# Gates folded into the experts' results, and the two rows of a token added by the second gather

## The chip, the core and the metric

The kernel runs on one core of a Trainium2 chip. The time is the device time of one execution in microseconds; the median of three executions of the kernel before is 1756.83 us (1756.41 to 1758.56). The engines are TensorE (PE in the profile; PEld is its loading of weights), VectorE (DVE), ScalarE (ACT), GpSimd (POOL) and SyncE (SP). POOL issues the indirect DMAs (gathers), SP and ACT issue the others.

## The reference

One layer of a model with 1024 tokens of width 1024: four attention-like branches, and then a mixture of 32 experts. The change concerns the mixture and the norm behind it:

```
h2 = rmsnorm(x2);  each token: a group by argmax, its two best experts e0, e1
gates g0, g1 = softmax(top 2) * softmax(group)          # per token
ys[e, slot] = (silu(h2 @ w1[e]) * (h2 @ w3[e])) @ w2[e]    # for the tokens of e
x2 = x2 + g0 * ys[row of (token, e0)] + g1 * ys[row of (token, e1)]
out = rmsnorm(x2) * final_norm_g
```

## The kernel before

All is float32; a matmul of the expert phase is made of three passes on values split in a high part (fp32r) and the remainder. `CAP` = 96 tokens of an expert form its block; tokens beyond 96 go to overflow blocks, whose code stands in a branch that is not taken with these inputs (`overflow`, L2461 on). The 32 experts are passed two at a time: experts 0 and 1 and experts 30 and 31 in code of their own, the others in a loop (`loop`, L2455). For an expert `e` = 2i + j:

- POOL copies the expert's token numbers and gathers 96 rows of `h2_rows` (`xg`); TensorE transposes them; ScalarE and VectorE make `xT_hi`, `xT_lo`.
- SP loads the weights; ScalarE makes the high part of each quarter, VectorE the remainder (`wa_lo` L2768, `wb_lo` L2776).
- TensorE runs the up projection in four quarters (`up`, 12 matmuls each), later the down projection (`down`, 24 matmuls). In between are ScalarE's sigmoid, VectorE's two products (`gl`, `hid`, L2762, L2764), TensorE's transposes of `hid` (L2410), and the split `hT_hi`, `hT_lo`.
- ScalarE copies the 96x1024 result from PSUM to `yo` (`y_out`, L2687) and stores it in `ys`, a DRAM tensor with 96 rows for each expert. For the last expert, 31, the down projection is done in two halves of 512 columns (L2564), each copied and stored at once (`y_end`).

VectorE works out where each token's two results lie (`blocks_of_experts` and what follows it); these row numbers are in `row_of`, and they hold overflow blocks too. The order on each engine is that of the code; there is no scheduler. Engines wait for one another by semaphores (`wait_ge`, `then_inc`), and `link` makes VectorE wait for its own last instruction.

`combine` is the end. POOL waits until every block is stored and then issues 16 gathers of 128 rows of 1024: for each tile `t` of 128 tokens one for the first expert (`ya`) and one for the second (`yb`). VectorE adds each to `x2[t]` multiplied by its gate (L2945, L2947). ScalarE squares and sums the tile (L2926) and takes the root (L2929); VectorE, after it has added the next tile, takes the reciprocal and multiplies by it and by the gain `fg` (L2938, L2939); SP stores the tile (L2906).

Of the kernel before, what the change touches and what calls it, by code (L numbers as in the profile page):

```python
# [49 lines left out]
SLOTS = (NE + N_OV) * CAP  # L50
# [42 lines left out]
def build(nc, a):  # L93

    ctx = ExitStack()
    with ctx:
# [89 lines left out]
        s.ys = dram("ys", [SLOTS, DM])  # L186
# [23 lines left out]
        s.row_of = sb("row_of", [P, 2 * NT], 202.125, I32)  # L210
        s.tok_of = sb("tok_of", [CAP, NE + N_OV], 202.25, I32)
        s.totals = sb("totals", [P, NE], 203)
        s.asg = sb("asg", [P, 8, 2, NT], 203.125)
        s.late_ready, s.routed = sem("late_ready"), sem("routed")
        s.late = {n: sb("late_" + n, shape, at) for n, shape, at in (
# [814 lines left out]
def attend(nc, a, s):  # L1030
# [136 lines left out]
    with nc.Block() as block:  # L1167
        @block.sync
        def _(sp):
# [16 lines left out]
            for k in range(2 * NGT):  # L1186
# [6 lines left out]
                if k in range(16, 30, 2):  # L1193
                    at = NE + (k - 16) // 2 * N_OV // 7
                    sp.wait_ge(zeros_ready, 1)
                    sp.dma_start(s.ys[at * CAP:(at + N_OV // 7) * CAP, :].rearrange("(b p) n -> p b n", p=CAP),
                                 zeros[:, :].unsqueeze(1).to_broadcast([CAP, N_OV // 7, DM])).then_inc(zeros_stored, 16)
                if k == 9:
                    sp.dma_start(bias[:, :, :], bass.AP(s.shifted.tensor, P - 1,
                                                        [[NH * 768 - 1, P], [768, NH], [1, BAND]])).then_inc(bias_in, 16)  # L1200
# [11 lines left out]
                if k == 56:  # L1212
                    sp.wait_ge(zeros_stored, 16 * 7)
# [656 lines left out]
def route(nc, a, s):  # L1870
# [24 lines left out]
    hot = sb("r_hot", [P, 2, NT, NE], 178)  # L1895
    both, cum = sb("r_both", [P, NT, NE], 180), sb("r_cum", [P, NT, NE], 181)
# [135 lines left out]
    def vector(dve):  # L2032
# [178 lines left out]
        nc.vector.tensor_copy(s.totals[:, :], psum[:, 4, 0:NE]).then_inc(s.routed, 1)  # L2211

# [122 lines left out]


# [3 lines left out]
def experts(nc, a, s):  # L2340
# [22 lines left out]
    OVER = 3  # L2363
    ov_set, over_ready, over_used, over_tok = sem("ov_set"), sem("over_ready"), sem("over_used"), sem("over_tok")
# [13 lines left out]
                                      "hid", "hT", "hT_taken", "y", "y_taken", "stored")}  # L2378
# [82 lines left out]
    def overflow(eng, body, before=None):  # L2461
# [3 lines left out]
        with eng.If(blocks > 0):  # L2465
            if before is not None:
                before()
            with eng.Fori(0, N_OV) as b:
                body(b)

    def expert_of(eng, b):
        return eng.value_load(s.ov_i[0:1, 0, bass.ds(b, 1)], min_val=0, max_val=NE - 1)

    def sync(sp):
# [15 lines left out]
        refill(NE // 2, 0, False, True)  # L2490

        def before():
            sp.wait_ge(ov_table, 1)
            sp.wait_ge(b_used, 2 * NE)

# [9 lines left out]
    def gpsimd(pool):  # L2505
# [16 lines left out]

        def before():
            pool.wait_ge(over_tok, 1)
            pool.wait_ge(b_used, 2 * NE)
            pool.sem_inc(ov["go"], 1)

# [7 lines left out]
        overflow(pool, body, before)  # L2535
        for j in range(2):
            pool.wait_ge(y_stored[j], 16 * (NE // 2 + j))

    def tensor(pe):
# [45 lines left out]
        def body(i, j, start, last):  # L2585
# [10 lines left out]
            if start:  # L2596
                pe.wait_ge(xT_low, 1)
                up(i, j, 2)
            if not last:
# [13 lines left out]
        down(NE // 2 - 1, 1, False, end=True)  # L2613

# [30 lines left out]
    def scalar(act):  # L2645
# [26 lines left out]
        def y_end(i):  # L2672

            act.wait_ge(y_stored[1], i * 16)
            for h in range(2):
                act.wait_ge(b_used, i * 4 + 3 + h)
                half = slice(h * 512, (h + 1) * 512)
                nc.scalar.activation(yo[1][:, half], y_banks(True)[:, h, :], ACT.Copy).then_inc(y_half, 1)
                act.wait_ge(y_half, h + 1)
                act.dma_start(s.ys[(i * 2 + 1) * CAP:(i * 2 + 2) * CAP, half], yo[1][:, half]).then_inc(y_stored[1], 16)  # L2680
# [11 lines left out]
        def body(i, j, start, last):  # L2692
# [32 lines left out]
            if last:  # L2725
                y_out(i, 0, False)
# [10 lines left out]
        y_end(NE // 2 - 1)  # L2737

        def before():
            for j in range(2):  # L2740
                act.wait_ge(y_stored[j], 16 * (NE // 2 + j))

        def body(b):
# [10 lines left out]
            act.dma_start(s.ys[bass.ds((b + NE) * CAP, CAP), :], yo[0][:, :]).then_inc(ov["stored"], 16)  # L2754
        overflow(act, body, before)

    def vector(dve):
# [28 lines left out]
        def blocks_of_experts():  # L2786
# [8 lines left out]
            link(nc.vector.tensor_tensor(cnt[:, 0, :], cnt[:, 2, :], cnt[:, 0, :], ALU.subtract))  # L2795
            some = many[:, 0:2 * NT, :]
            link(nc.vector.tensor_tensor(some, line(0).unsqueeze(2).to_broadcast([P, 2 * NT, MORE]),
                                         late["steps"][:, :].unsqueeze(1).to_broadcast([P, 2 * NT, MORE]),
                                         ALU.is_ge))
            link(nc.vector.tensor_reduce(out=line(3), in_=some, axis=AX.X, op=ALU.add))  # L2800
            link(nc.vector.scalar_tensor_tensor(out=line(4), in0=line(3), scalar=-float(CAP), in1=line(0),
                                                op0=ALU.mult, op1=ALU.add))
            link(nc.vector.tensor_scalar(line(6), line(3), 1.0, None, ALU.min))
            every = [P, 2 * NT, NE]
            link(nc.vector.tensor_tensor(hot2[:, :, :], late["e"][:, :].unsqueeze(1).to_broadcast(every),
                                         line(1).unsqueeze(2).to_broadcast(every), ALU.is_equal))
# [206 lines left out]
```

## Time and profile before

| | |
|---|---|
| median of three runs | 1756.83 us |
| the profiled execution | 1755.01 us |
| its span (first to last instruction of the profile) | 1753.2 us |
| TensorE busy | 1682.4 us, 96% |
| VectorE busy | 1440.0 us, 82% |
| ScalarE busy | 938.5 us, 54% |
| POOL busy | 137.5 us, 8% |
| chain of waits: TensorE's L2548 and L2580, the expert projections | 20% and 10% of the span |
| the expert phase, by the first matmul of expert 0 | from about 1140 us |

A profile is one execution recorded by the hardware. A busy share is an average over phases with different limits. The chain of waits goes back from the last instruction to whatever released it; it tells which engine set the end. A timeline row gives start, length, engine, line, operation, and the tiles written and read; in square brackets stands how long the engine had been idle and what released it. Ends of matmuls are modelled: a record of 0.39 us belongs to matmuls that start 0.23 us apart.

### The profile page before, as it was taken

To read this page: it belongs to the slowest core of one execution; us is meant where nothing else is said; L and a number is where in the kernel's file an instruction comes from. 1 tells how busy PE (TensorE), PEld (TensorE's weight loads), DVE (VectorE), ACT (ScalarE), POOL (GpSimd) and SP (SyncE) were. 2 spreads that over 40 slices of the span, in tenths; PEclk is the share of its full clock that TensorE was granted. 3 is DMA by queue.
4 is the path that set the end of the run, shared out by engine and by line. 5 is a ranking of instruction groups with operands and counts; after the bars stand their busy time and mean duration, and the time that the engine had idled before them with its cause. 6 is when DMAs were issued, how large, how long until landed. Compare 5 with 4: busy or idle time off the path is not lost. (4 is left out here: it accounts for less than half of the span.)

```text
span 1753.2 us, 24115 instructions
## 1 busy us (share of the span) xinstructions
PE 1682.4 (96%) x8776; PEld 1271.4 (73%) x8776; DVE 1440.0 (82%) x2045; ACT 938.5 (54%) x1218; POOL 137.5 (8%) x137
## 2 busy tenths in 40 slices
PE   7999999999999999999999999999999999999990
PEld 7768888877777777777777778867777777777760
DVE  6587958989789988678737986789998989898997
ACT  6533122133444555545566542177778787777762
POOL 1100000000000000000000000032212111100003
PEclk9999999999999999999999999999999999999995
DMA  5202122122354412412315942399999999999977
GB/s 210 72 1 85 54 103 97 61 79 79 111 193 124 147 61 67 144 55 69 124 37 199 329 167 83 121 381 392 402 395 405 393 404 394 403 395 403 402 281 287
DMA packets 77040, 359.82 MB, mean 205 GB/s; under 512 B 9020, under 2 KB 11612, under 8 KB 50588
## 3 DMA queue, kind: packets, MB, share of 16 engines
q1 hardware_dynamic: 67372, 325.14, 49.7%
q0 software_dynamic: 5888, 20.97, 3.6%
q10 hardware_dynamic: 3696, 12.59, 1.8%
q8 instruction: 53, 0.87, 0.2%
q14 instruction: 31, 0.25, 0.0%
HBM read 301.63 MB, written 55.99 MB: 204 GB/s over the span
## 5 line engine op out<-in xcount | busy, mean ns | idle before, releaser
L2768 DVE TENSOR_TENSOR wa_lo<-wa,w_hi 128x2048 fp32r<-128x2048 f32 x124 | 280.9, 2283 | 14.8 <-ACT w_hi L2652 14.1
L2652 ACT ACTIVATE w_hi<-wa 128x2048 fp32r<-128x2048 f32 x124 | 237.6, 1917 | 75.8 <-DMA wa<-expert_up 54.5
L1583 PE MATMUL psum<-h_hi,w_hi 128*128 128x512 f32 x512 | 210.4, 411 | 2.1 <-ACT gate_out L1245 1.6
L1583 PE MATMUL psum<-h_hi,w_lo 128*128 128x512 f32 x512 | 204.3, 399 | 0.0
L1583 PE MATMUL psum<-h_lo,w_hi 128*128 128x512 f32 x512 | 202.3, 395 | 0.0
L175 DVE MAX8 top<-sel 128x8 f32<-128x384 f32 (+5 forms) x192 | 171.2, 892 | 4.6
L173 DVE MATCH_REPLACE8 sel<-top,sel 128x384 f32<-128x384 f32 (+5 forms) x192 | 168.1, 875 | 0.0
L2776 DVE TENSOR_TENSOR wb_lo<-wd,w_hi 128x2048 fp32r<-128x2048 f32 x62 | 139.3, 2288 | 30.6 <-ACT w_hi L2662 30.6
L2548 PE MATMUL psum<-w_hi,xT_hi 128*96 128x512 f32 x508 | 162.1, 400 | 0.0
L2548 PE MATMUL psum<-wa_lo,xT_hi 128*96 128x512 f32 x512 | 159.8, 393 | 0.0
L2548 PE MATMUL psum<-w_hi,xT_lo 128*96 128x512 f32 x508 | 158.6, 393 | 0.0
L1583 PEld LDWEIGHTS psum<-h_hi,w_hi 128*128 128x128 f32 x512 | 96.3, 188 | 49.9 <-issue 16.8
L1262 ACT ACTIVATE pt<-psum 128x512 f32<-128x512 f32 (+3 forms) x144 | 61.1, 470 | 116.5 <-PE psum L1603 116.4
L2662 ACT ACTIVATE w_hi<-wd 128x2048 fp32r<-128x2048 f32 x62 | 116.0, 1909 | 0.7 <-PE psum L2548 0.5
L969 PE MATMUL psum<-h_hi,w_hi 128*128 128x512 f32 x288 | 115.0, 399 | 0.0
L1583 PEld LDWEIGHTS psum<-h_hi,w_lo 128*128 128x128 f32 x512 | 96.2, 188 | 24.8 <-issue 5.1
L969 PE MATMUL psum<-h_hi,w_lo 128*128 128x512 f32 x288 | 112.5, 391 | 0.0
L969 PE MATMUL psum<-h_lo,w_hi 128*128 128x512 f32 x288 | 112.2, 390 | 0.0
L1583 PEld LDWEIGHTS psum<-h_lo,w_hi 128*128 128x128 f32 x512 | 96.4, 188 | 19.8 <-issue 2.7
L2548 PEld LDWEIGHTS psum<-wa_lo,xT_hi 128*96 128x96 f32 x512 | 82.6, 161 | 35.5
L2548 PEld LDWEIGHTS psum<-w_hi,xT_lo 128*96 128x96 f32 x508 | 82.1, 162 | 35.2
L2548 PEld LDWEIGHTS psum<-w_hi,xT_hi 128*96 128x96 f32 x508 | 77.4, 162 | 27.0 <-issue 0.2
(398 smaller groups left out, 3296.6 us busy)
## 6 DMA issues: line engine op xcount, KB each, us to landing
wa<-expert_up SPq DMA_DIRECT2D x128, 1024.0 KB, 23.4
wd<-expert_down SPq DMA_DIRECT2D x64, 1024.0 KB, 23.6
w<-w_gate SPq DMA_DIRECT2D x32, 512.0 KB, 4.2
gate_pre<-gate_out SPq DMA_DIRECT2D x64, 256.0 KB, 3.5
gate<-gate_pre SPq DMA_DIRECT2D x32, 512.0 KB, 5.9
ys<-yo ACTq DMA_DIRECT2D x31, 384.0 KB, 7.0
w<-w_T SPq DMA_DIRECT2D x18, 512.0 KB, 3.7
ys<-zeros SPq DMA_DIRECT2D x7, 1152.0 KB, 5.9
```

The costliest lines, as they stand in the source:

```text
L173: link(nc.vector.match_replace(sc, top8[:, :], sc, TAKEN))
L175: link(nc.vector.max(top8[:, :], sc))
L969: ins = nc.tensor.matmul(psum[:, bank + h, :], w[:, k, :], x[:, k, h * 512:(h + 1) * 512], start=(k == 0 and r == 0), stop=(k == KC - 1 an ...
L1262: nc.scalar.activation(dst, src, ACT.Copy).then_inc(pt_copied, 1)
L1583: ins = nc.tensor.matmul(psum[:, 7, :], w[:, k, :], x[:, k, half * 512:(half + 1) * 512], start=(n == 0), stop=(n == BURST - 1))
L2548: ins = nc.tensor.matmul(psum[0:CAP, up_bank(i, j) + m, :], x[:, k, :], w[:, c, m, :], start=(k == 0 and x is xT_hi[j] and w is not wa_lo[ ...
L2652: nc.scalar.activation(hi_a(i, j, q).rearrange("p c m n -> p (c m n)"), wa[j][q][:, :, :, :].rearrange("p c m n -> p (c m n)"), ACT.Copy). ...
L2662: nc.scalar.activation(dst.rearrange("p f n -> p (f n)"), wb[j][q][:, :, :].rearrange("p f n -> p (f n)"), ACT.Copy).then_inc(b_high, 1)
L2768: nc.vector.tensor_tensor(wa_lo[j][q][:, :, :, :].rearrange("p c m n -> p (c m n)"), wa[j][q][:, :, :, :].rearrange("p c m n -> p (c m n)" ...
L2776: nc.vector.tensor_tensor(wb_lo[j][q][:, :, :].rearrange("p f n -> p (f n)"), wb[j][q][:, :, :].rearrange("p f n -> p (f n)"), high.rearra ...
```

## The change

1. *Gates.* At the end of the routing VectorE multiplies the one-hot table of each token's experts by the gates and splits it in two (`hot_g`). TensorE sums it over the tokens with 16 small matmuls (`slot_gates`), and the result, `slot_gate`, holds for each expert and each of its 96 slots the gate of the token there. ScalarE's copies of results out of PSUM now multiply by it.
2. *Row numbers.* They are worked out early, before VectorE's last weight subtractions, and only for the first 96 tokens of experts 0 to 29 (`early_rows`). A token whose expert is 30 or 31, or that has overflowed, gets the number of a row of zeros. Overflow blocks have a tensor of their own, `ys_ov`, gathered and added inside the branch that is not taken.
3. *Gathers.* POOL issues eight gathers for the tokens' first experts into eight buffers `rows_of`, as soon as expert 29 is stored and the buffer is free, then eight for the second experts, which add to the same buffers in memory (`compute_op=ALU.add`).
4. *Experts 30 and 31* (`LATE` = 2) are not stored. ScalarE writes the high part of the gated result (`yl_hi`), VectorE the remainder (`yl_lo`), and TensorE puts them in their tokens' places by one-hot matrices `hotT` that compare a running number with the expert's token numbers: eight matmuls of 512 columns a tile.
5. *Sums.* VectorE adds TensorE's tile from PSUM to `x2[t]`, and then the buffer `rows_of[t]`. For tiles 2 and 3 (`ON_PE`) TensorE adds the buffer instead, by two plain float32 matmuls with the identity, so that VectorE adds once.
6. *The end.* All eight tiles are summed before the first is multiplied. The gain is loaded and the square root's table set earlier; `out` has buffers of its own.

```diff
         def body(i, j, start, last):          # pool: behind the loop
+        pool.wait_ge(a_used, 4 * (NE - 1))
+        pool.iota(tok_iota[:, 0:ZERO_ROW], ...)
+        pool.iota(tok_iota[:, ZERO_ROW:], ...).then_inc(iota_set, 1)
+        s.set_eps(pool)
+        pool.wait_ge(s.rows_set, 1)
+        for j in range(2):
+            pool.wait_ge(y_stored[j], 16 * (NE // 2 - 1))
+        for k in range(2):
+            for t in range(NT):
+                ...
+                if k:
+                    pool.wait_ge(s.rows_in[t], 16)
+                    pool.indirect_dma_start(rows_of[t][:, :], None, s.ys, at, compute_op=ALU.add
+                                            ).then_inc(s.rows_in[t], 16)
+                else:
+                    if t >= 2:
+                        pool.wait_ge(a_used, 4 * (NE - 1) + (2 if t < 6 else 3))
+                    pool.indirect_dma_start(rows_of[t][:, :], None, s.ys, at).then_inc(s.rows_in[t], 16)
...
+        def late(t, k):                        # tensor
+            for h in range(2):
+                if t == 0:
+                    pe.wait_ge(late_low, k + 1 + k * h)
+                for r, y in enumerate((yl_hi[k], yl_lo[k])):
+                    ins = nc.tensor.matmul(psum[:, late_banks(t) + h, :], hotT[k][:, t * P:(t + 1) * P],
+                                           y[:, h * 512:(h + 1) * 512], ...)
+            if k == LATE - 1 and t in ON_PE:
+                pe.wait_ge(s.rows_in[t], 32)
+                for h in range(2):
+                    ins = nc.tensor.matmul(psum[:, late_banks(t) + h, :], s.ident[:, :],
+                                           rows_of[t][:, h * 512:(h + 1) * 512], start=False, stop=True)
+            if k == LATE - 1:
+                ins.then_inc(late_ready, 1)
+        late(0, 0)
+        late(1, 0)
+        late(0, 1)
+        late(1, 1)
+        for t in range(2, NT):
+            if t >= 4:
+                pe.wait_ge(s.summed if t - 4 in ON_PE else late_taken, t - 3)
+            for k in range(LATE):
+                late(t, k)
...
-            nc.scalar.activation(yo[j][:, :], y_banks().rearrange("p a b -> p (a b)"),
-                                 ACT.Copy).then_inc(y_taken, 1)
+            nc.scalar.activation(yo[j][:, :], y_banks().rearrange("p a b -> p (a b)"), ACT.Copy,
+                                 scale=s.slot_gate[:, bass.ds(i * 2 + j, 1)]).then_inc(y_taken, 1)
...
+        def late_adds():                       # vector
+            taken = 0
+            for t in range(NT):
+                dve.wait_ge(late_ready, t + 1)
+                at = late_banks(t)
+                ins = nc.vector.tensor_tensor(s.x2[t][:, :], psum[:, at:at + 2, :].rearrange("p a b -> p (a b)"),
+                                              s.x2[t][:, :], ALU.add)
+                if t in ON_PE:
+                    ins.then_inc(s.summed, 1)
+                    continue
+                taken += 1
+                ins.then_inc(late_taken, 1)
+                dve.wait_ge(late_taken, taken)
+                dve.wait_ge(s.rows_in[t], 32)
+                nc.vector.tensor_tensor(s.x2[t][:, :], rows_of[t][:, :], s.x2[t][:, :], ALU.add
+                                        ).then_inc(s.summed, 1)
...
-        for t in range(NT):                    # combine, vector
-            x2 = s.x2[t][:, :]
-            dve.wait_ge(y_in[t], 32)
-            link(nc.vector.scalar_tensor_tensor(out=x2, in0=ya[t][:, :], scalar=s.gates[:, 0, t:t + 1], in1=x2,
-                                                op0=ALU.mult, op1=ALU.add))
-            link(nc.vector.scalar_tensor_tensor(out=x2, in0=yb[t][:, :], scalar=s.gates[:, 1, t:t + 1], in1=x2,
-                                                op0=ALU.mult, op1=ALU.add))
-            nc.vector.engine_nop().then_inc(summed, 1)
-            if t:
-                finish(t - 1)
-        finish(NT - 1)
+        for t in range(NT):
+            dve.wait_ge(rooted, t + 1)
+            link(nc.vector.reciprocal(rms[:, t:t + 1], rms[:, t:t + 1]))
+            nc.vector.scalar_tensor_tensor(out=out[t][:, :], in0=s.x2[t][:, :], scalar=rms[:, t:t + 1],
+                                           in1=fg[:, :], op0=ALU.mult, op1=ALU.mult).then_inc(final, 1)
```

On VectorE, the end of the program before: `x` is the tile of the running sum, `ya` and `yb` the gathered rows.

```order
L2945 SCALAR_TENSOR_TENSOR x_0_9500<-ya_10668,gates,x_0_9500 128x1024
L2947 SCALAR_TENSOR_TENSOR x_0_9500<-yb_10676,gates,x_0_9500 128x1024
L2949 ISA
L2945 SCALAR_TENSOR_TENSOR x_1_9501<-ya_10669,gates,x_1_9501 128x1024
L2947 SCALAR_TENSOR_TENSOR x_1_9501<-yb_10677,gates,x_1_9501 128x1024
L2949 ISA
L2938 RECIPROCAL rms_10687<-rms_10687 128x1
L2939 SCALAR_TENSOR_TENSOR ya_10668<-x_0_9500,rms_10687,fg 128x1024
```

The same place on VectorE in the changed program, behind the last difference `yl_lo` of expert 31; `rows_of` are the gathered buffers.

```order
L2951 SCALAR_TENSOR_TENSOR yl_lo_10686<-psum,slot_gate,yl_hi_10676 96x512
L2960 TENSOR_TENSOR x_0_9502<-psum,x_0_9502 128x1024
L2969 TENSOR_TENSOR x_0_9502<-rows_of_10677,x_0_9502 128x1024
L2960 TENSOR_TENSOR x_1_9503<-psum,x_1_9503 128x1024
L2969 TENSOR_TENSOR x_1_9503<-rows_of_10678,x_1_9503 128x1024
L2960 TENSOR_TENSOR x_2_9504<-psum,x_2_9504 128x1024
L2960 TENSOR_TENSOR x_3_9505<-psum,x_3_9505 128x1024
L2960 TENSOR_TENSOR x_4_9506<-psum,x_4_9506 128x1024
L2969 TENSOR_TENSOR x_4_9506<-rows_of_10681,x_4_9506 128x1024
```

Two gated additions and a product per tile have become two plain additions (one for tiles 2 and 3), and the products stand behind all of them.

On POOL, the end of the program before, from the last gather for the loop to the first four of the end.

```order
L2508 DMA xg_9545<-h_rows,idx_10658 96x1024
L2464 TENSOR_LOAD ov_i
L2464 ISA x2
L2465 COMPARE_AND_BRANCH
...
L2911 MEMSET eps_10688 128x1
L2916 DMA ya_10668<-ys,row_of 128x1024
L2916 DMA yb_10676<-ys,row_of 128x1024
L2916 DMA ya_10669<-ys,row_of 128x1024
L2916 DMA yb_10677<-ys,row_of 128x1024
```

And in the changed program; L2605 are the plain gathers, L2600 those that add.

```order
L2570 DMA xg_9549<-h_rows,idx_10663 96x1024
L2587 IOTA tok_iota 96x768
L2588 IOTA tok_iota 96x256
L2525 MEMSET eps_10692 128x1
L2605 DMA rows_of_10677<-ys,row_of 128x1024
L2605 DMA rows_of_10678<-ys,row_of 128x1024
L2605 DMA rows_of_10679<-ys,row_of 128x1024
...
L2600 DMA rows_of_10677<-ys,row_of 128x1024
L2600 DMA rows_of_10678<-ys,row_of 128x1024
...
L2508 TENSOR_LOAD ov_i
L2508 ISA x2
L2509 COMPARE_AND_BRANCH
```

The 16 gathers have moved ahead of the overflow branch and of the stores of experts 30 and 31, and the two of a tile no longer stand side by side: all plain ones come first.

## Rows read from the trace of the kernel before

**Rows 1.** Chain that ended last, from 1690: start us, us, what

```profile
1701.01 5.58 PE psum L2564 x24
...
1711.53 5.36 DMA yb<-ys,row_of
...
1716.99 1.29 DVE x L2945
```

**Rows 2.** Timeline, one tile near the end: start us, us, engine, line, operation, tiles

```profile
1738.69 0.16 DVE L2938 RECIPROCAL rms<-rms 128x1 f32<-128x1 f32 x1
...
1738.89 1.28 DVE L2939 SCALAR_TENSOR_TENSOR ya<-x,rms,fg 128x1024 f32<-128x1024 f32 x1
...
1748.52 1.28 DVE L2939 SCALAR_TENSOR_TENSOR ya<-x,rms,fg 128x1024 f32<-128x1024 f32 x1
```

**Rows 3.** The tile out, its last two stores

```profile
DMA to landing us min/median/max: 2.9/3.1/3.3
```

**Rows 4.** Windows: from:to, length, busy us by engine, granted clock, DMA share, GB/s

```profile
1710.00:1710.50 0.50, 0.00 (x0) 0.00 (x0) 0.00 (x0) 0.00 (x0) 0.24 (x1) 0.89 0.00 0
...
1720.00:1724.00 4.00, 0.00 (x0) 0.00 (x0) 3.77 (x5) 3.85 (x7) 3.09 (x4) 0.50 1.01 407
```

**Rows 5.** Timeline, VectorE, TensorE at expert 31's down projection

```profile
1696.94 0.69 DVE L2764 TENSOR_TENSOR hid<-psum,gl 96x512 f32<-96x512 f32 x1
1697.55 2.28 DVE L2776 TENSOR_TENSOR wb_lo<-wd,wa_lo 128x2048 fp32r<-128x2048 f32 x1
1697.69 0.55 PE L2410 MATMUL psum<-ident,hid 96*128 96x96 f32 x4
```

**Rows 6.** Timeline of VectorE before and after it

```profile
1689.36 4.50 DVE L2776 TENSOR_TENSOR wb_lo<-wd,w_hi 128x2048 fp32r<-128x2048 f32 x2 [0.62 <-ACT w_hi L2662]
1693.78 2.28 DVE L2776 TENSOR_TENSOR wb_lo<-wd,wa_lo 128x2048 fp32r<-128x2048 f32 x1
...
1700.22 0.48 DVE L2788 TENSOR_TENSOR l_many<-totals,late_steps 128x320 f32<-128x320 f32 x1
```

**Rows 7.** Groups by form, VectorE and TensorE: count, busy us, mean ns

```profile
L2039 DVE TENSOR_TENSOR x<-psum,x 128x512 f32<-128x512 f32 x16 | 11.0, 691 | 17.3 <-PE psum L1701 17.3
L2768 DVE TENSOR_TENSOR wa_lo<-wa,w_hi 128x2048 fp32r<-128x2048 f32 x124 | 280.9, 2283 | 14.8 <-ACT w_hi L2652 14.1
L177 DVE TENSOR_SCALAR sel<-sel 128x1024 f32<-128x1024 f32 x1 | 0.7, 694 | 0.0
L1524 PE MATMUL psum<-k,q 64*128 64x512 f32 x88 | 24.3, 637 | 0.0
```

**Rows 8.** The tile ys, the store of expert 29 at 1686.6

```profile
DMA to landing us min/median/max: 7.0/7.0/7.0
```

**Rows 9.** Timeline, VectorE and POOL at two places

```profile
1162.92 4.48 DVE L2776 TENSOR_TENSOR wb_lo<-wd,w_hi 128x2048 fp32r<-128x2048 f32 x2
1163.39 4.83 POOL L2508 DMA_INDIRECT xg<-h_rows,idx  x1 [0.80 <-POOL idx L2517]
...
1717.74 1.35 POOL L2916 DMA_INDIRECT ya<-ys,row_of  x1 [0.31 <-issue]
1718.31 1.28 DVE L2947 SCALAR_TENSOR_TENSOR x<-yb,gates,x 128x1024 f32<-128x1024 f32 x1
...
L2916 POOL DMA_INDIRECT yb<-ys,row_of x8 | 8.0, 997 | 2.4 <-issue 2.4
```

**Rows 10.** Timeline of ScalarE, last half of expert 31

```profile
1706.61 0.59 ACT L2678 ACTIVATE yo<-psum 96x512 f32<-96x512 f32 x1 [2.13 <-PE psum L2564]
```

**Rows 11.** Timeline of TensorE near the program's start

```profile
13.59 0.43 PE L839 MATMUL psum<-w_lo,h_hi 128*128 128x268 f32 x1
...
17.39 0.29 PE L839 MATMUL psum<-w_hi,h_hi 128*128 128x268 f32 x1
```

**Rows 12.** Timeline of TensorE, first two experts

```profile
1148.48 0.63 PE L2548 MATMUL psum<-w_hi,xT_lo 128*96 128x512 f32 x2
1150.96 0.88 PE L2404 MATMUL psum<-ident,xg 96*128 96x96 f32 x8 [1.85 <-DMA xg<-h_rows,tok_of]
```

More of the change, by code:

```diff
@@ L2334, in tensor, with slot_gates @@
         s.late_tokens = late_tokens
+        def slot_gates():
+            pe.wait_ge(s.gates_set, 1)
+            for k in range(2):
+                for t in range(NT):
+                    ins = nc.tensor.matmul(psum[0:CAP, 3, 0:2 * NE], hot_c[:, k, t, :],
+                                           hot_g[:, k * NT + t, :, :].rearrange("p r e -> p (r e)"),
+                                           start=(k == 0 and t == 0), stop=(k == 1 and t == NT - 1))
+            ins.then_inc(s.gates_summed, 1)
+        s.slot_gates = slot_gates
     return Engines(sync=sync, gpsimd=gpsimd, scalar=scalar, vector=vector, tensor=tensor)
@@ L2534, in body @@
             pool.sem_inc(ov["go"], 1)
-        overflow(pool, body, before)
-        for j in range(2):
-            pool.wait_ge(y_stored[j], 16 * (NE // 2 + j))
+        overflow(pool, body, before, then)
     def tensor(pe):
@@ L2736, in scalar @@
         loop(act, body)
[L2737 to L2741, printed above, removed]
+        y_late(1)
+        nc.scalar.activation(table[:, :], s.totals[:, 0:1], ACT.Sqrt)
         def body(b):
@@ L2801, in blocks_of_experts, with late_rows @@
-            link(nc.vector.scalar_tensor_tensor(out=line(4), in0=line(3), scalar=-float(CAP), in1=line(0),
-                                                op0=ALU.mult, op1=ALU.add))
[L2803 to L2806, printed above, removed]
+        def late_rows():
+            link(nc.vector.tensor_copy(tok_f[:, :], s.tok_of[:, NE - LATE:NE]))
+            dve.wait_ge(iota_set, 1)
+            for k in range(LATE):
+                nc.vector.tensor_scalar(hotT[k][:, :], tok_iota[:, :], tok_f[:, k:k + 1], None, ALU.is_equal
+                                        ).then_inc(late_hot, 1)
@@ L2881, in body, with then @@
             glu(ov["half"], b + 1).then_inc(ov["hid"], 1)
-        overflow(dve, body, before)
+        def then():
+            for n in range(2 * NT):
+                t, k = n // 2, n % 2
+                dve.wait_ge(ov_in[k], 16 * (t + 1))
+                if k:
+                    dve.wait_ge(ov_added, n)
+                nc.vector.scalar_tensor_tensor(out=s.x2[t][:, :], in0=ov_rows[k][:, :],
+                                               scalar=s.gates[:, k, t:t + 1], in1=s.x2[t][:, :], op0=ALU.mult,
+                                               op1=ALU.add).then_inc(ov_added, 1)
+            dve.wait_ge(ov_added, 2 * NT)
+        overflow(dve, body, before, then)
     return Engines(sync=sync, gpsimd=gpsimd, tensor=tensor, scalar=scalar, vector=vector)
```

231 lines of the change are left out of this document (164 added, 67 removed).

## The prediction, made before the result was known

> **What bounds the kernel now.** I read the page's busy shares first, then the chain of waits, and last the timeline of the final 60 us. TensorE is 96% busy, and inside the expert loop the chain never leaves it: up to the last matmul of expert 31 the time is TensorE's. That ends when 24 matmuls of the last down projection, 0.2325 us apart, have run (1701.01 + 5.58 = 1706.6) [rows 1]. Then come two things that are not TensorE's. First a gap of 10.4 us: the result is copied and stored, POOL starts its 16 gathers only after that store, and the first pair is there when the chain leaves the second gather, begun at 1711.53 and 5.36 us long, so VectorE starts at 1716.99 [rows 1]. Then VectorE alone: 8 tiles in 1749.80 - 1716.99 = 32.8 us, of which the reciprocal and the last product are 1740.17 - 1738.69 = 1.48 us a tile, and the two gated additions are the rest, 2.6 us a tile [rows 2]. After 1748.52 + 1.28 = 1749.80 the last store takes 3.3 us [rows 3]; the span ends 3.4 us after VectorE. So 46.6 us of the 1753.2 lie behind TensorE's last matmul, and all that the change can win is there.
>
> **The change, part by part.**
>
> *Start of the experts.* VectorE gets four instructions behind the totals (two of 256, two of 512 elements, at most 0.69 us each by the 512-element addition [rows 7], so under 2.5 us), and TensorE 16 small matmuls behind expert 0's third quarter. TensorE stands there anyway: it is through with the quarter at about 1149.1, and the next instruction begins at 1150.96, 1.85 us later, waiting for rows of expert 1 [rows 12]. At the price of the eight transposes behind that wait (8 in 0.88 [rows 12]) 16 take 1.8 us. Cost 0; bounds 0 and 0.9 us, half of them uncovered. VectorE's two quarters move from 1143.7 to 1146 and are needed at 1151.6 and later: nothing. ScalarE's copies only gain a scale operand: nothing, it waits elsewhere.
>
> *Row numbers for experts 0 to 29.* Five dependent instructions of 16 elements before VectorE's last subtractions; at a reciprocal's 0.16 us plus a gap of 0.04 [rows 2] they take 1.0. The subtraction behind them waited 0.62 us for ScalarE [rows 6], so VectorE is 0.4 late; the subtraction of 1693.78 ended at 1696.06, and the two products that end in the gated rows began about 1696.2, so 0.15 of that is absorbed [rows 5, 6]. TensorE's transposes begin at 1697.69, right behind that product's end at 1697.63 [rows 5], and nothing else is in its queue ahead: TensorE's end moves by 0.3, to 1706.9. Bounds 0 and 0.4.
>
> *Experts 30 and 31 no longer go through memory.* Behind TensorE's end come ScalarE's half copy, 0.59 [rows 10], and VectorE's difference, 0.7, but TensorE fills that time: it owes tiles 0 and 1 their expert 30 part first. 8 matmuls of 0.2325 bring it to 1708.8, four more finish tile 0 at 1709.7 plus a tail of 0.16, and VectorE can begin at 1709.9 instead of 1716.99. TensorE has tiles 1 and 2 (without its rows) done at 1712.5. The block count (first instruction 0.48 [rows 6]) stands between VectorE's two half differences, under a half projection of 12 x 0.2325 = 2.8 us: free.
>
> *VectorE's own work.* An addition of 1024 elements: between 691 ns at 512 and 2283 ns at 2048 [rows 7], that is 1.22, with its gap 1.25. There are 14 (two a tile, one for tiles 2 and 3): 17.5 us. Products with reciprocal: 8 x 1.48 = 11.8. Together 29.3 against 32.8. All sums now come before the first product, so the root of a tile is long there; the stores then come every 1.48 us, and the last two stores of before, that close together, landed after 2.9 to 3.3 us [rows 3]. I keep 3.4.
>
> *The gathers.* Here lies the price that decides. All 16 are issued by POOL as before; eight plain, then eight that add. The first waits for expert 29's store, issued at 1686.6 and landed 7.0 us later, at 1693.6 [rows 8]. Unhindered, a gather is 1.0 us with 0.3 between two [rows 9]. But in the loop POOL's gather begun at 1163.39 lasts 4.83 us: it ends at 1168.2, one gather's length after VectorE's pair of subtractions ends at 1167.40. In the tail the gather begun at 1717.74 is only 1.35 long, though a 1.28 us product starts at 1718.31 and isn't stretched [rows 9]. I read: a gather that begins inside a VectorE instruction with two operands in SBUF waits for a gap between two such, and once begun holds nobody up. By that reading the first gather waits for the subtraction of 1693.8, now 0.4 later, until 1696.5 and ends at 1697.4; the second ends at 1698.7; the third waits for the last weight subtraction until 1700.1 and ends at 1701.0; the fourth for the two one-hot comparisons (0.69 each [rows 7]) until 1702.4; the next four follow at 1.3. The first adding gather is issued at 1708.8 and, at 5.4 to landing [rows 1], is there at 1714.2; those of tiles 1, 2, 3 at 1715.5, 1716.8, 1718.1.
> A rule of the Trainium skill stands beside this reading (SBUF — State Buffer, section "SBUF: two separate sides"): VectorE with two SBUF inputs and a GpSimd instruction that reads SBUF take a shared port pair exclusively, for the whole instruction, whoever is first. The wait for VectorE agrees with 4.83 us; the other half, VectorE held for a whole gather, does not, since its products stay at 1.28 us in the midst of the gathers, and by it the end would come up to 8 us later than below, if each of the eight late gathers held VectorE for 1.0.
>
> *The sum.* VectorE adds tile 0's sum from 1709.9 to 1711.2 and waits for rows until 1714.2. Then tile 0 to 1715.5, tile 1 to 1718.0. Tile 2's rows come through TensorE by an identity: a plain float32 matmul of 512 columns is 637 ns long in the record [rows 7], so 0.47 apart if its tail is the usual 0.16; two end at 1717.8, and VectorE is done at 1719.2. TensorE has tile 3 at 1717.8 + 1.9 + 0.94 = 1720.6, VectorE takes it to 1722.0; tile 4 is ready at 1722.6, and four tiles at 2.5 end at 1732.6. With 11.8 and 3.4 the span ends at 1747.8, against 1753.2. In one line: VectorE starts 7.1 us earlier, has 3.5 less work, and loses 5.1 in waits (3.0 for tile 0's rows, 1.5 and 0.6 for tiles 3 and 4), so about 5.4 are gained. The profiled execution is 1755.01, 1.8 above its span and 1.8 below the median of 1756.83; the difference carries over: 1756.83 - 5.4 = 1751.4.
> Bounds. Below: no gather is held up and rows are never late; tile 3 is then ready at 1712.5 + 0.94 + 1.9 + 0.94 + 0.16 = 1716.4, tile 4 at 1718.2, VectorE's last addition ends at 1728.2 and the span at 1743.4. Above: TensorE idles from 1712.5 to 1716.8. In the profile its clock fell about 3.8 us after the last matmul (1706.6 to the half-lowered stretch 1710.0 to 1710.5 [rows 4]). At 1.2 GHz its prices double; at the start of the program matmuls that began at 13.2 without a pause were long, 0.43, until 17.2 and 0.29 from then [rows 11], so I take 4 us of the low level: tile 3 is 1.9 later, the end 1749.7.
>
> **Rivals.**
> *Gathers in time.* If POOL's waits are rarer than I think, the lower bound holds: 1756.83 - 9.8 = 1747.0. For it: in the tail only a few tenths were lost per gather. Against: 4.83 us in the loop, and three subtractions of that kind in POOL's way.
> *TensorE stays at the low level.* Tile 2's two take 1.9 then, to 1718.7; tile 3's eight 3.7 and its two 1.9, to 1724.3; after it a tile comes every 3.7 us, tile 7 at 1739.1; end 1739.1 + 2.5 + 11.8 + 3.4 = 1756.8, time 1760.4. For it: the gap in which it falls. Against: from there on TensorE works without a pause.
> *The other side: a gather that adds is much dearer than a plain one.* No row shows one. At 407 GB/s and full DMA share [rows 4] half a megabyte is 1.3 us; bounds for one that adds are 1.3, the plain price, and 3.9, if reading the rows, reading the buffer and writing it came one after another. The first lands at 1716.5 then, the eighth 7 steps later, and VectorE adds it, 1.25, before the products. From a step of 2.9 us on the kernel is slower than before; at 3.9 the end is 1743.8 + 1.25 + 11.8 + 3.4 = 1760.3, the time 1763.9. At 2.6 (1758.3) it is still no change. I take 1.3, since the eight can overlap and at that price they keep ahead of VectorE's 2.5 us a tile.
>
> **How the numbers follow.** My forecast 0.45 (its own range 1749 to 1755), gathers in time 0.30, low clock throughout 0.08, dear adding gathers 0.17, a third of it at 2.6 or less. A measurement tells 0.2%, 3.5 us, from no change: faster means under 1753.3. Nine tenths of the forecast and all of the second: 0.69. Slower, over 1760.3: most of the dear gathers and half of the low clock, 0.15; the rest 0.16. Range 1745 to 1760.
>
> **What would show it.** Right: TensorE's last projection ends near 1706.9; VectorE's first addition from PSUM near 1710 and a wait of 2 to 4 us for an adding gather behind it; eight plain gathers on POOL, two or three of 2 to 3 us; the product phase 11.8 us long and all in one piece. Wrong: VectorE waits for adding gathers at tiles 4 to 7 too (they are dear), or for TensorE at each tile (clock), or additions stretched above 1.3 us, or the expert loop longer than before.

## The result, and the profile after

The changed kernel takes 1760.56 us (median of 20 runs), the kernel before 1757.75 (20 runs): ratio 1.0014, 95% interval 1.0008 to 1.0020. It is a little slower, inside the 0.2% that I had called no change, and above my range of 1745 to 1760. The profiled execution has a span of 1761.0 us. One of the changed kernel's 20 executions took 5956 us, which nothing here explains; it is left out of the ratio and doesn't move the median.

The 7.8 us between the two spans lie in two places. Take the end of TensorE's last projection product, by its record, as the mark: in the kernel before it was at 1706.6 (1701.01 + 5.58 [rows 1]), 46.6 us ahead of the end of the span. After:

```profile
1712.96 0.39 PE L2656 MATMUL psum<-wa_lo,xT_lo 128*96 128x512 f32 x1
1713.19 0.40 PE L2714 MATMUL psum<-yl_hi,hotT 96*128 96x512 f32 x1
```

These are rows of the timeline (start, duration, engine, line, operation). The last projection product ends at 1713.35, 6.8 us later than before; the first product of the late experts follows it without a gap. From the mark to the end it is 47.7 us, where I had forecast 40.9 and the kernel before has 46.6.

**Ahead of the experts.** This is the granted clock in the routing stage (windows: TensorE busy, instructions, clock, DMA share, GB/s):

```profile
1126.00:1130.00 4.00, 4.00 (x22) 1.00 0.33 98
1134.00:1138.00 4.00, 4.00 (x22) 0.50 0.87 367
1142.00:1146.00 4.00, 4.00 (x24) 0.50 1.00 414
1146.00:1150.00 4.00, 4.00 (x13) 0.50 0.76 280
1150.00:1154.00 4.00, 4.00 (x17) 0.90 0.68 198
```

From about 1134 to 1151 TensorE ran at its lower level, 1.2 GHz (0.50). In the profiled execution of the kernel before it stayed at 2.4 GHz:

```profile
1140.00:1144.00 4.00, 4.00 (x23) 1.00 1.02 408
1144.00:1148.00 4.00, 4.00 (x19) 1.00 1.02 368
```

There [rows 12] show TensorE waiting 1.85 us for the rows of expert 1. In the chain of waits after, there is no such wait:

```profile
1146.76 10.33 PE psum L2640 x36
1157.09 1.31 PE psum L2359 x16
1158.40 0.72 PE psum L2448 x8
```

The 36 products of the up projection run into the 16 gate products (L2359), and those into the transposes: the gate products are 1.31 us of the path.

**Behind the experts.** The waits between 1705 and 1750 (engine, tile and line, released by, total, times, longest):

```profile
PE psum L2720 <- DMA rows_of<-ys,row_of: 8.5, 1, 8.5
DVE x L2960 <- PE psum L2720: 7.5, 2, 5.1
DVE x L2969 <- DMA rows_of<-ys,row_of: 4.9, 1, 4.9
```

VectorE waits 4.9 us for tile 0's rows and 7.5 us for TensorE, which itself stood 8.5 us for tile 2's rows. The chain of waits through it:

```profile
1718.01 9.23 DMA rows_of<-ys,row_of
1727.25 0.04 issue
1727.29 3.78 PE psum L2720 x4
1731.07 1.92 PE psum L2714 x8
1732.99 1.72 PE psum L2720 x4
1734.71 1.85 PE psum L2714 x8
1736.58 1.24 DVE x L2960
...
1746.67 0.17 DVE rms L3124
```

Tile 2's adding gather starts at 1718.01, its rows are there 9.2 us later. The identity products (L2720, four records a tile) then take 3.78 us for tile 2 and 1.72 for tile 3. The gathers on POOL:

```profile
1699.28 2.37 POOL L2605 DMA_INDIRECT rows_of<-ys,row_of  x1 [13.13 <-DMA ys<-yo]
1701.95 1.87 POOL L2605 DMA_INDIRECT rows_of<-ys,row_of  x1 [0.30 <-issue]
1704.13 3.21 POOL L2605 DMA_INDIRECT rows_of<-ys,row_of  x1 [0.30 <-issue]
...
1713.00 0.94 POOL L2605 DMA_INDIRECT rows_of<-ys,row_of  x1 [0.30 <-issue]
1714.25 1.59 POOL L2600 DMA_INDIRECT rows_of<-ys,row_of  x1 [0.30 <-issue]
1716.14 1.56 POOL L2600 DMA_INDIRECT rows_of<-ys,row_of  x1 [0.30 <-issue]
```

On POOL a plain one is 0.94 long when nothing holds it up, one that adds 1.55. What follows lies in the DMA engines, by the windows while nothing but adding gathers runs:

```profile
1722.00:1724.00 2.00, 0.00 (x0) 0.50 1.04 207
1724.00:1726.00 2.00, 0.00 (x0) 0.50 1.08 215
```

At full DMA share the adding gathers deliver 207 to 215 GB/s, half of what the plain gathers of [rows 4] do at 407.

### The profile page after: what moved, and what is told of

It is laid out like the page before. It is cut to its first block and busy times, and to the rows that moved or that the text cites. A ratio compares the mean times of both kernels' runs of the same rounds, so it can differ in the third digit from the quotient of the medians.

```text
span 1761.0 us, 24321 instructions
## 1 busy us (share of the span) xinstructions
PE 1711.3 (97%) x8864; PEld 1293.3 (73%) x8864; DVE 1438.1 (82%) x2042; ACT 947.3 (54%) x1221; POOL 170.1 (10%) x139
```

## The experiments

Theory: the tail is long because adding gathers take the DMA engines twice as long and land late, and because tiles 2 and 3 go through TensorE. The rival was that the time was lost upstream by the clock. Each median is of 5 to 12 runs, and each ratio is to runs of the kernel before taken beside them: 35 (medians 1757.72, 1757.94) or 17 (1757.37). "Tail" is from the mark to the end of the span, in the one profiled execution of each; the changed kernel's first profile had 47.7. A and B below are the theory and the rival of each experiment's own expectation.

| kernel | median us | ratio to before | tail us |
|---|---|---|---|
| before, again | 1757.08 | 0.9994 (0.9985 to 1.0003) | 46.6 |
| changed, again | 1759.52 | 1.0009 (1.0000 to 1.0017) | 47.0 |
| vector_adds_all | 1754.82 | 0.9985 (0.9976 to 0.9994) | 44.1 |
| plain_second_gather | 1757.12 | 0.9997 (0.9988 to 1.0006) | 45.1 |
| gathers_interleaved | 1757.43 | 0.9991 (0.9982 to 1.0000) | 44.5 |
| interleaved_vector_adds | 1756.38 | 0.9984 (0.9975 to 0.9992) | 43.2 |
| one_gate_product | 1758.99 | 1.0006 (0.9997 to 1.0015) | 48.0 |
| tensor_kept_busy | 1758.29 | 1.0003 (0.9994 to 1.0012) | 45.5 |
| standstills_filled | 1758.69 | 1.0010 (1.0001 to 1.0019) | 50.1 |
| half_the_adding | 1752.48 | 0.9965 (0.9953 to 0.9977) | 41.0 |
| half_the_adding_odd | 1752.16 | 0.9965 (0.9952 to 0.9979) | 40.2 |

**The kernel before, again** (no edit).

> The kernel before, once more, for its granted clock. Theory A (the fall of TensorE's clock to 0.50 between 1134 and 1150 us, which cost the profiled execution of the changed kernel 6.9 us, comes now and then in either kernel): this look may show it or not; the mean granted clock of its executions scatters from 0.983 to 0.988, and the slowest are those with the lowest clock. Rival B (only the changed kernel has it): the clock is 1.00 from 1120 to 1160 us again, and all executions have 0.988.

Its windows:

```profile
1134.00:1138.00 4.00, 3.06 (x28) 1.00 0.81 340
1138.00:1142.00 4.00, 4.00 (x23) 0.52 0.94 307
1142.00:1146.00 4.00, 4.00 (x18) 0.50 1.01 422
1146.00:1150.00 4.00, 4.00 (x14) 0.70 0.88 297
```

The low level is here too, from 1138 to about 1148, and TensorE's last projection ends at 1709.4, 2.8 us later than in the first profile, with the same tail. So B is out: the kernel before has the fall as well. Of the 35 executions of the kernel before that ran beside it, two have a mean granted clock of 0.988, the value of the execution that I had studied, with spans of 1752.4 and 1752.9; the other 33 have 0.981 to 0.987 and 1754.1 to 1760.2. That the profile I predicted from was a rare one fits this, and the 1.8 us by which it lay under the median; how rare isn't shown, for a mean counts falls anywhere, and this execution has another one (granted clock 0.86 from 456 to 460 us and 0.71 from 460 to 464). Of the 13 profiled executions here, nine have the fall in the routing stage.

**VectorE adds all rows.**

```
-    ON_PE = (2, 3)
+    ON_PE = ()
```

> The changed kernel, but VectorE also adds the gathered rows of tiles 2 and 3 (two additions of 1.23 us more), and TensorE has no identity product. Theory A (the tail is long because tile 2's rows come late and their price on TensorE is 3.8 us at the low clock, and tiles 3 and 4 queue behind that): VectorE waits for rows at tile 0 only, then runs 16 additions in one piece, last addition 4 to 5 us earlier against TensorE's last projection, time 0.2 to 0.3% under the changed kernel. Rival B (the adding gathers' own pace is the bound, about 2.5 us from landing to landing): VectorE waits again at tiles 2 and 3 for rows, and no more than 1 us is won. Rival C (the time is set upstream, by TensorE's low clock in the routing stage, and the tail hardly counts): the time stays within 1 us of the changed kernel's unless the granted clock from 1132 to 1150 us stays at 1.00.

The time is 5.7 and 4.7 us under the changed kernel's two medians, at A's upper end or above it, and the tail 2.9 to 3.6 shorter. VectorE waited four times for rows:

```profile
DVE x L2969 <- DMA rows_of<-ys,row_of: 7.2, 4, 6.3
```

Tile 0 is 6.3 of it, the other three 0.9 in all. From then on the rows come just as fast as VectorE adds, and the DMA engines are full all the while, at half the rate of a plain gather:

```profile
1725.00:1727.00 2.00, 2.00 (x10) 1.00 1.06 211
1727.00:1729.00 2.00, 1.12 (x5) 1.00 1.06 211
1729.00:1731.00 2.00, 0.00 (x0) 1.00 1.06 211
```

512 KB at 211 GB/s are 2.48 us a gather. So A is right on TensorE's detour and on what is won, and B on the gathers' pace alone. The profiled execution had no clock fall in the routing stage; the 16 gate products then lie in a wait for expert 1's rows, of which 1.5 us are left, and TensorE's last projection ended at 1708.0, 1.4 later than in the first profile of before, since those rows came 1.5 later.

**The second gather plain.**

```
-                    pool.indirect_dma_start(rows_of[t][:, :], None, s.ys, at, compute_op=ALU.add
+                    pool.indirect_dma_start(rows_of[t][:, :], None, s.ys, at
```

> The changed kernel, but the second gather of each tile overwrites the buffer instead of adding to it, so the first expert's row of each token is left out of the sum. Theory A (a gather that adds is the dear thing: 1.55 us on POOL against 0.94, and some 8 us from issue to landing against 5.4): POOL's second eight are 0.94 long with 0.3 between, tile 0's rows are there 5.4 us after the issue, so VectorE's wait at tile 0 falls from 4.9 to about 2.5 us and TensorE's for tile 2's rows from 8.5 to about 4; the end comes 3 to 5 us earlier. Rival B (the landing is late because VectorE or the weight loads' traffic hold the gathers, whatever they do with the buffer): the second eight land as late as before, 8 to 9 us after issue, and the time is the same.

```profile
1717.00:1719.00 2.00, 0.00 (x0) 0.56 1.02 418
1719.00:1721.00 2.00, 0.00 (x0) 0.50 1.02 412
```

Double the rate at the same share: 1.25 us a gather. The tail is 45.1 against 47.0 and 47.7: 1.9 to 2.6 us for the adding, less than A's 3 to 5. One part of A fell: the first of these gathers (issued at 1711.43) served VectorE only at 1718.6, 7.1 us later; VectorE's wait at tile 0 was 5.3, not 2.5, and TensorE's for tile 2 was 6.3, not 4. The first adding gather of the changed kernel took 8.1 (1714.25 to 1722.33), so most of what is over 5.4 isn't the adding.

**Another order on POOL.**

```
+        order = ((0, 0), (0, 1), (0, 2), (0, 3), (1, 0), (1, 1), (0, 4), (1, 2), (0, 5), (1, 3), (0, 6), (1, 4),
+                 (0, 7), (1, 5), (1, 6), (1, 7))
+        for k, t in order:
```

> The changed kernel with another order on POOL: plain gathers of tiles 0 to 3, then adding and plain ones in turn (tile 0, 1, then 4, 2, 5, 3, ...), so that tile 0's adding gather is issued about 5 us earlier. Theory A (an adding gather has a latency of 8 us, and the wait for the first is what is lost): VectorE's wait at tile 0 goes from 4.9 to under 1 us, TensorE's wait for tile 2's rows from 8.5 to about 4 us, and the time falls by 3 to 5 us. Rival B (the engines of the DMA rings are the bound, 16 gathers and the last stores sharing them): the last rows land no earlier, and VectorE only waits at a later tile; under 1 us.

VectorE's wait at tile 0 is gone, TensorE's for tile 2 is 5.2 instead of 8.5. The median is 3.1 and 2.1 us under the two of the changed kernel: A, at its lower end or just under it.

**Both edits together.**

> The changed kernel with both edits of the first experiments: POOL issues adding gathers in turn with the later plain ones, and VectorE adds the rows of all eight tiles. Theory A (an adding gather occupies the DMA engines for 2.46 us where a plain one takes 1.25, so the 16 need some 30 us of them; VectorE's 16 additions and 8 products are the other limit): rows of tile 0 are there when TensorE's sum is, VectorE waits 2 to 4 us in all for later rows, from TensorE's last projection to the end of the span 39 to 41 us against 47.7 of the changed kernel, 44.0 and 44.5 of the two single edits; time 6 to 8 us under the changed kernel and 3.5 to 5 under the kernel before. Rival B (latency of each adding gather, not the engines' time): no wait behind the first tile, 38 us. Rival C (both single edits removed the same wait): 43 to 44 us.

Rival C: 43.2, no faster in the median than VectorE's adding alone. VectorE waits for rows at five tiles, and POOL, ahead of four adding gathers, for the plain gather into the same buffer:

```profile
DVE x L2970 <- DMA rows_of<-ys,row_of: 6.3, 5, 2.1
POOL rows_of L2601 <- DMA rows_of<-ys,row_of: 7.3, 4, 2.2
```

VectorE's sum is only 0.9 under the 7.2 above. POOL's waits leave the DMA engines no gap, though; from 1714 to 1734 their share is 1.02 or more in every stretch of 4 us, as in this one (here the busy time is VectorE's):

```profile
1722.00:1726.00 4.00, 2.36 (x2) 1.00 1.05 277
```

So an earlier first gather hardly brings the last rows earlier.

**One gate product instead of 16.**

```
-            for k in range(2):
-                for t in range(NT):
-                    ins = nc.tensor.matmul(psum[0:CAP, 3, 0:2 * NE], hot_c[:, k, t, :],
+            ins = nc.tensor.matmul(psum[0:CAP, 3, 0:2 * NE], hot_c[:, 0, 0, :],
```

> The changed kernel with one product for the slots' gates at the start of the experts instead of 16, so all gates but those of token tile 0's first choice are left out. Theory A (where TensorE's clock falls to 0.50 in the routing stage, its wait for rows of expert 1 is used up, and the 16 products cost their whole 1.31 us): with such a fall, from the start of the products of oh_late to the first transposes of expert 0's hidden rows it takes 1.2 us less than in the changed kernel at the same fall, about 26.0 instead of 27.2; without a fall there is a wait 1.2 longer and no gain. Rival B (the products are covered anyhow): no difference in either.

Its clock fell from 1138 to 1148, and its chain reads:

```profile
1137.52 3.28 PE psum L2287 x16
...
1154.23 0.03 PE psum L2357
1154.26 0.69 PE psum L2445 x8
1154.95 8.31 PE psum L2637 x36
1163.27 0.33 PE psum L2451 x4
```

From 1137.52 to 1163.27 it is 25.75 us; with 16 products and a fall of the same length 27.03 in plain_second_gather (1136.34 to 1163.37) and 27.03 in tensor_kept_busy (1137.02 to 1164.05). A holds: 1.28 us, uncovered.

**TensorE kept at work in the wait for tile 2.**

```
+                if t == 2:
+                    for n in range(34):
+                        nc.tensor.matmul(psum[:, 0, :], hotT[0][:, 0:P], yl_hi[0][:, 0:512], start=True, stop=True)
                 pe.wait_ge(s.rows_in[t], 32)
```

> The changed kernel with 34 extra products of 512 columns into a free bank while TensorE waits for tile 2's rows (7.9 us of the 8.5 it stood). Theory A (half of the identity products' 3.78 us for tile 2 is the low clock after the standstill): the granted clock stays at 1.00 until the last product, tile 2's identity products take 1.7 to 1.9 us, tile 3's eight products 1.85 instead of 2.0, and VectorE's last addition comes 1.9 to 2.1 us earlier against TensorE's last projection; time 1.5 to 2 us under the changed kernel. Rival B (what is late at tile 2 is the rows alone, and tile 4 to 7 are then bound by VectorE's own start): under 0.5 us.

```profile
1714.63 8.98 DMA rows_of<-ys,row_of
...
1723.65 1.98 PE psum L2723 x4
1725.64 1.83 PE psum L2714 x8
1727.47 1.72 PE psum L2723 x4
```

1.98 instead of 3.78 us, with 0.5 us of standstill left and the granted clock at 1.00 throughout; the tail is 1.5 to 2.2 shorter and the time 1.2 and 2.3 under the changed kernel's. A holds.

**The changed kernel, again** (no edit).

> The changed kernel once more. Theory A (TensorE's clock falls to 0.50 in the routing stage in nearly every execution of either kernel, as the mean clock of the kernel before's executions says, 0.988 in 2 of 35 and less in the others): a fall of 8 to 16 us somewhere from 1132 to 1152 us again; from TensorE's last projection to the end of the span 47.7 us again; adding gathers land 2.5 us apart. Rival B (the long tail of the first look was its own): a tail under 46.6.

The clock was 0.50 from 1138 to 1145, 7 us and not 8 to 16, and the tail 47.0. Both of the changed kernel's tails are above 46.6, this one by 0.4; B is out.

**The standstills of the routing stage filled.**

```
+        def busy(n):
+            for _ in range(n):
+                nc.tensor.matmul(psum[:, 3, 0:4 * CAP], hot_m[:, 0, 0:4, :].rearrange("p t e -> p (t e)"),
+                                 hot_c[:, 0, 0:4, :].rearrange("p t e -> p (t e)"), start=True, stop=True)
...
+        busy(2)
         logits(NT - 1, 1)
...
+        busy(5)
         pe.wait_ge(oh_ready, 3)
```

> The changed kernel with seven extra products of 384 columns in the routing stage, two ahead of the last logits (TensorE stands there 0.3 us) and five ahead of the last products of oh_late (0.9 us); their result is not used. Theory A (TensorE's clock falls to 0.50 at 1134 to 1138 us because TensorE stands still for 1.2 us there): the granted clock stays at 1.00 from 1130 to 1152 us, the time comes 2.5 to 4 us earlier. Rival B (it falls for another reason, the many products of 36 to 128 columns or something outside the program): the fall is there again and the time is that of the changed kernel, or up to 0.3 us more.

Inconclusive on the clock, and against A on the time. The clock stayed at 1.00 in the profiled execution, but so it did in three without the filling (the first of before, vector_adds_all, half_the_adding_odd), and the time is only 0.8 and 1.9 us under the two medians of the changed kernel. What it shows is where a saved fall goes:

```profile
1694.67 2.74 POOL L2612 DMA_INDIRECT rows_of<-ys,row_of  x1 [15.01 <-DMA ys<-yo]
```

The last projection ended at 1706.9, so POOL's first gather comes 12.2 us ahead of it; in the changed kernel's first profile it was 14.1 (1699.28 and 1713.35). From the issue of expert 29's store to this gather it is 7.6 us (1687.05), against 5.7 there (1693.55). That the weight loads keep their own time and hold the store back is my reading; for it speaks that ScalarE waits 28 to 69 times for an expert's weights in the four profiles without the fall and at most 12 times in the nine with it. The first adding gather is then issued 2.1 us behind the mark (1708.99), where the changed kernel's two profiles have 0.9; TensorE stands 10.2 us for tile 2's rows, and the tail grows to 50.1.

This bears on two rows of the table. In vector_adds_all and plain_second_gather, too, the second gathers start 2.1 us behind the mark (1710.12 and 1711.43). Against this one profile, which shares the late start, their tails are 6.0 and 5.0 us shorter, so the 2.9 to 3.6 and 1.9 to 2.6 above are rather too low; which of the two is the larger stays the same.

**Half of the adding taken away.**

```
+    BY_PE = (4, 5, 6, 7)
+    rows_b = {t: sb(f"rows_b{t}", [P, DM], 128 + 4 * n) for n, t in enumerate(BY_PE)}
...
+            if k and t in BY_PE:
+                pool.wait_ge(b_used, 2 * (NE - 1))
+                pool.indirect_dma_start(rows_b[t][:, :], None, s.ys, at).then_inc(rows_b_in[t], 16)
...
-            if k == LATE - 1 and t in ON_PE:
-                pe.wait_ge(s.rows_in[t], 32)
+            if k == LATE - 1 and t in BY_PE:
+                pe.wait_ge(s.rows_in[t], 16)
```

> The changed kernel with the interleaved order on POOL, and adding gathers for tiles 0 to 3 only; of tiles 4 to 7 both gathers are plain, each into its own buffer, TensorE adds the first (identity, in the tile's PSUM sum, after a wait that is over long before), VectorE the second. VectorE's additions stay at 16. Theory A (the DMA engines' time is the bound of interleaved_vector_adds: 8 x 1.25 + 8 x 2.46 = 29.7 us; here 12 x 1.25 + 4 x 2.46 = 24.8): VectorE's waits for rows fall from 6.3 to 1 or 2 us, from TensorE's last projection to the end of the span 38 to 39.5 us against 43.1, the time 3.5 to 5 us under that kernel's 1756.4. Rival B (each row set's latency behind POOL's waits is the bound): the waits stay at 5 to 6 us, 42 to 43. Rival C (TensorE becomes the bound: 3.6 us a tile from tile 4 on, more after a fall of its clock): VectorE waits for TensorE at tiles 5 to 7, 40 to 42.

> As half_the_adding, but the four tiles with two plain gathers are 1, 3, 5 and 7 instead of 4 to 7. Theory A (DMA engines' time): the rows of tiles 2 and 3, which VectorE needs first, come 1.2 and 2.4 us sooner, so the waits at the early tiles shrink; 38 to 39 us from TensorE's last projection to the end. Rival C (TensorE): its identity products for tile 1 (1.72 us) and 3 delay tile 2, but VectorE takes 2.5 us a tile, so no wait is added. If both variants end within 0.5 us of each other, VectorE's own 31 us is the bound.

Both build on interleaved_vector_adds: the order on POOL is the same, and `ON_PE` is empty. For four tiles (`BY_PE`; 1, 3, 5 and 7 in the second) both gathers are plain, TensorE adds the first by the identity and VectorE the second. Both beat both kernels: 1752.48 and 1752.16 (7 and 5 runs), 0.35% under the kernel before, and 3.9 and 4.2 us under interleaved_vector_adds. VectorE's waits for gathered rows in the first and the second:

```profile
DVE x L2979 <- DMA rows_of<-ys,row_of: 3.7, 2, 2.1
DVE x L2979 <- DMA rows_b<-ys,row_of: 0.4, 2, 0.2
```

```profile
DVE x L2979 <- DMA rows_of<-ys,row_of: 3.3, 3, 1.4
DVE x L2979 <- DMA rows_b<-ys,row_of: 0.2, 1, 0.2
```

They are 4.1 and 3.5 us instead of 6.3, and none is for TensorE's identity: A by its cause, but the tails are 1.5 and 1.2 us over A's, since the wait left is again for the adding gathers. C is out. POOL's waits of 7.3 us went too, to none and 3.2, so B isn't shut out by this pair alone; against it stands the full DMA share of interleaved_vector_adds.

## Why the prediction was wrong

Its times in us behind the mark, the end of TensorE's last projection, as forecast and as in the profile after:

| | forecast | after |
|---|---|---|
| VectorE's first addition | 3.0 | 2.9 (1716.24) |
| tile 0's rows | 7.3 | 9.0 (1722.33) |
| tile 2's rows | 9.9 | 13.9 (1727.25) |
| tile 2 through TensorE | 10.9 | 17.7 (1731.07) |
| tile 3 through TensorE | 13.7 | 21.4 (1734.71) |
| VectorE's last addition ends | 25.7 | 32.9 (1746.25) |
| end of the span | 40.9 | 47.7 |

*Right.* TensorE's order behind its last product and VectorE's start stand to 0.1 us, VectorE's prices too (an addition 1.22, with its gap 1.25; the products 0.5 less in all), and so do the plain gathers held up by VectorE's instructions with two operands in SBUF: three of 2.37, 1.87 and 3.21 us. The first adding gather was issued at 1714.25, 0.9 behind the mark where I had 1.9. By the Trainium skill (SBUF — State Buffer, section "SBUF: two separate sides") a gather would also hold VectorE for its whole length; VectorE's addition of 1722.33 began inside POOL's gather of 1721.72, which is 1.55 long, and took 1.23 us all the same, so that half again doesn't show here.

*The step that failed: "I take 1.3, since the eight can overlap and at that price they keep ahead of VectorE's 2.5 us a tile."* Adding gathers do overlap in flight, issued 1.9 us apart and 8 us long, but the DMA engines are full with them: one takes 2.48 us there, not 1.3. Tile 2's rows came 4.0 us late. The two steps from tile 0's rows to tile 2's (4.92 us, 2.46 each) are 2.3 of it. The other 1.7 is the landing, 2.7 longer than forecast, less the 1.0 by which the first was issued earlier. I took 5.4 us, the first gather on idle engines [rows 1]; the adding ones took

```profile
DMA to landing us min/median/max: 8.0/8.3/8.6
```

while a plain one in their place served VectorE after 7.1. The kernel before already had a median of 6.2 us and a longest of 9.8 for `yb`. Behind tile 2 the adding gathers made VectorE wait no more in the changed kernel; what stood in the way there was TensorE.

A dear adding gather was the rival that I gave 0.17, but it isn't vindicated either. At a step of 2.6 its own terms give 1716.5 + 7 x 2.6 + 1.25 + 11.8 + 3.4 = 1751.2 and a time of 1754.8, not the 1758.3 that I wrote; by them a step of 2.48 alone would have left the kernel faster than before. The case nearest in number, TensorE at the low level throughout (1760.4), is near by luck: behind tile 2 the granted clock is back at 1.00, and VectorE waits 2.4 us for tile 3 and 0.6 for tile 4, not for every tile. My share for "faster" was mis-added too (0.9 x 0.45 + 0.30 is 0.71, not 0.69).

The Trainium skill (Collectives: The Full Stack, section "Stop ④ — SDMA + CCE: where bytes move and the add happens") calls the addition itself free in a collective's transfer, but counts two reads and one write for it. The doubled time here agrees with the second read; no run separates the read from the addition.

*The identity products: 0.94 us a tile, measured 1.72.* I read a record of 637 ns as one matmul. A float32 matmul of 512 columns leaves two records, 0.43 apart, so it is 0.86 against 0.2325 of an fp32r one. The ratio of 3.7 is near the Trainium skill's four passes for true FP32 (FP8 and Floating Point Precision, section "TensorE Precision Notes"). Another 2.06 for tile 2 is the low clock after 8.5 us of standstill, by the 1.98 us that tensor_kept_busy has in its place; I had that as an upper bound of 1.9 in all. VectorE adding all rows took 2.9 to 3.6 us off the tail, more than plain gathers did (1.9 to 2.6): TensorE's detour was the dearer half.

*The start of the experts: "Cost 0; bounds 0 and 0.9".* 1.31 us (1.30 in one), in every profiled execution with a clock fall and all 16 products. The cover was a wait that no execution with the fall has. I had not asked what the cover was worth in the median execution, though the profile lay 1.8 us under the median.

*The sum.* The tail is 0.4 to 1.1 us longer instead of 5.7 shorter, and 1.3 at the start: 1.7 to 2.4 us slower, where the medians say 2.8 and 1.6. My 5.4 us of gain against 2.8 of loss differ by 8.2: 6.8 in the tail, 1.3 at the start. Within the 6.8, rows of tile 2 are 4.0 late, its products 2.8, tile 3 0.8, and 0.8 is won back behind it. The 6.8 us by which the mark lies later in the profile after are, beside this 1.3, a clock fall of 17 us; the kernel before has such falls as well, so I don't count them in the change. Open stays what makes the clock fall in the routing stage; what TensorE did before it, products of 36 to 128 columns with standstills of 0.3 and 0.9 us, is the same work with the fall and without it. Not tried: two plain gathers for all tiles, which needs four more buffers and more of TensorE.

## What to carry to other kernels

Where a transfer takes over an addition, price it in the DMA engines' time as well as on the issuing engine, and take a landing time from gathers in a full queue, not from the first. Before a cost is set to nothing because a wait covers it, ask whether the typical execution has the wait: a profile under the median of its runs is a warning. A tail measured from an engine's last product moves with what starts before that product, so compare two profiles where the transfers begin at the same distance from it. Work handed to an idle engine costs what it waits for, plus the low clock after the wait; give it inputs that are there long before, as the last two versions do.

## What the runs showed of the hardware

- A gather of 128 rows of 4 KB that adds to its buffer in SBUF moved 207 to 215 GB/s at full DMA share, a plain one 412 to 418; on POOL they are 1.55 and 0.94 us.
- TensorE's clock fell to 0.50 for 7 to 17 us in the routing stage in nine of 13 profiled executions, of either kernel, and not in the others; one of the four without it had seven products added to that stage.
- A fall there is partly given back. From expert 1's first transposes to the mark it is 554.9 to 555.0 us in the nine profiles with the fall and 555.3 to 557.9 in the four without. With the same code at the end, the tail was 50.1 without a fall and 47.0 and 47.7 with falls of 7 and 17 us, so it doesn't follow the fall's length.
- Gathers on POOL that met VectorE's subtractions with two operands in SBUF lasted 2.37, 1.87 and 3.21 us instead of 0.94; VectorE's additions of that kind kept 1.22 to 1.23 us beside gathers.
